# Prompt attention with operands split in pieces twelve steps ahead, its first pair loaded during decode, and the new tokens of the local sets multiplied together

## The chip, the cores and the metric

The program runs on one core of one Trainium2 chip, and its time is the device time of one execution in microseconds (us). The core has TensorE (PE, with its weight loads shown as PEld), VectorE (DVE), ScalarE (ACT), GpSimd (POOL) and SyncE (SP), which issues nearly all the transfers here. Each engine works through its own list of instructions in order and waits on semaphores that the others raise.

## What is computed

One layer of a hybrid decoder: a prompt of 512 positions, and 8 sequences of 8 new tokens with 4096 cached positions each. Both go through an input projection, attention in four sets of heads (one forgetting attention, "FOX", and three dilated sliding windows, "WIN", that are merged by their softmax denominators), gates and an MLP.

```python
q_f, k_f, v_f, logf, dil, ga, gb = project(h_p, pos_p, lp)
o_fox = fox_prompt(q_f, k_f, v_f, logf)
for g, ((w, r), (q, k, v)) in enumerate(zip(DIL_PATTERNS, dil)):
    o, lse = dilated_prompt(q, k, v, w, r)
h_p = finish(h_p, o_fox, merge_groups(outs, lses), ga, gb, lp)
...
q_f, k_f, v_f, logf, dil, ga, gb = project(h_s, pos_s, lp)
k_past = cache_fox_k[l][page_table].reshape(DB, past, N_HEADS_FOX, HEAD_DIM)
v_past = cache_fox_v[l][page_table].reshape(DB, past, N_HEADS_FOX, HEAD_DIM)
o_fox = fox_sample(q_f, k_f, v_f, logf, k_past, v_past, f_past)
o, lse, new_buf = dilated_sample(q, k, v, win_caches[g][l], w, r)
h_s = finish(h_s, o_fox, merge_groups(outs, lses), ga, gb, lp)
```

## The kernel before

The kernel has four parts, one after another, with a barrier of all engines between them: `project_tokens`, `attend_sample` (the decode part), `attend_prompt` and `finish`. To keep float32 accuracy every operand of a matmul is split into a high and a low part (`x_hi` by a copy on ACT, `x_lo` = x minus `x_hi` on DVE or POOL), and a product is made of two or three matmuls.

**Decode part.** For each of the 8 sequences ("batches") the cache is worked through in 24 groups: 16 FOX groups of 256 positions and 8 WIN groups (sets 1, 2, 3) of 128 or 256 gathered positions. `straight` writes the stages of each engine out by hand: at step n (24 steps for a batch) PE turns the keys of group n (L1211), turns probabilities of group n-21 (L1188), scores group n-2 (L1227) and sums values of group n-22 (L1242); SP loads keys for n and values for n-20, into rings of 6 slots each. The 8 new tokens of a sequence are appended to the last group of each of the four sets (`group_new`: groups 15, 16, 18 and 23). For such a group PE also turns an 8-column piece of `prob` (L1191) and adds two matmuls of 8 rows by 512 columns from `vn_hi` and `vn_lo` (the last loop of `sum_values`). POOL loads `vn_hi` and `vn_lo` once a batch, in two transfers. The FOX output and the merged WIN output of a batch are scaled on DVE (`out_rows`), turned on PE (`turn_out`, L1203) and copied into `o_t` (`out_diagonal`). After the last one SP stores `o_t` to `o_s` and waits for it.

**Prompt part.** The heads are taken in 4 pairs. A pair is 32 chunks: 2 heads, 4 query tiles, 4 sets in `SET_ORDER`; a chunk has 1 to 4 key tiles of 128. The steps of the `stream` of each engine are chunks too: PE scores chunk n-4 (L1599), turns the probabilities of chunk n-16 (L1611) and weighs the values of chunk n-18 where the query tile is the last (L1632). DVE keeps and masks the scores of chunk n-5 (L1554), takes the maximum and its negative (L1565, L1567), makes reciprocals and `pt_lo` (L1579). ACT takes exponentials (L1490), normalises FOX (L1497) and makes `pt_hi` (L1505); POOL normalises WIN (L1451). There are three banks for scores and three for turned probabilities, so PE can be at most three chunks ahead of DVE. The operands of a pair are split at fixed steps of it, four and more steps ahead of their use:

```python
if i in (0, 8):
    ...
    ve.tensor_tensor(q_lo[rows, hh], q_raw[rows], q_hi[rows, hh].bitcast(F32), ALU.subtract).then_inc(q_split, 1)
if 1 <= i <= SETS:
    ...
    ve.tensor_tensor(k_lo[:, s], k_raw[:, s], k_hi[:, s].bitcast(F32), ALU.subtract).then_inc(k_split, 1)
```

ACT does the `_hi` parts at the same steps (L1474, L1479) and `v_hi` at step 18 (L1483), POOL `v_lo` (L1444). `k_hi` and `k_lo` have one buffer, so a set's keys for the next pair can be split only when its last chunk (28 to 31) has been scored. At the start of the part SP loads `q_raw` and `k_raw` of the first pair (1 MB each), the biases, `causal`, `masks`, the values and two slabs for `finish`, in that order; the stored decode outputs come back into `o_all` last.

## Time and profile before

| | |
|---|---|
| median of 3 runs | 1935.24 us (1931.7 to 1937.51) |
| the profiled execution | 1934.01 us, span 1932.2 us |
| mean granted TensorE clock | 0.961 |
| busy share PE, DVE, ACT, POOL | 92%, 57%, 49%, 43% |

The table is the whole program; the parts differ, so a table by stage is among the rows below. The span is what the trace covers, 1.8 us less than the execution's own time. A busy PE is not PE at its peak, since the ends of matmuls are modelled; the distance between the starts of two matmuls is what one costs.

### The profile page before, as it was taken

What the parts mean: (1) busy time and instruction counts of PE and PEld (TensorE: products, weight loads), DVE (VectorE), ACT (ScalarE), POOL (GpSimd) and SP (SyncE); (2) the same over time, 40 slices, a digit from 0 to 9 for tenths busy, and PEclk for the clock granted to TensorE, in tenths of its full rate; (3) what the DMA queues carried; (4) which work ended last, traced back from release to release, by engine and by line L of the source; (5) the groups of instructions that cost most, each with busy time, mean ns of one, the idle gap of its engine ahead of it and who ended that gap; (6) DMA issues with size and microseconds to landing.
All of it is one profiled execution on the core that took longest, in us unless ns stands there. A gap on an engine that the chain in (4) does not pass through costs nothing. (4 is left out here: it accounts for less than half of the span.)

```text
span 1932.2 us, 33076 instructions
## 1 busy us (share of the span) xinstructions
PE 1771.0 (92%) x10797; PEld 1556.2 (81%) x10797; DVE 1107.8 (57%) x2535; ACT 954.2 (49%) x1608; POOL 830.4 (43%) x449
## 2 busy tenths in 40 slices
PE   7999999999599999999999947877799799999998
PEld 5787787899587888888888726777698799989897
DVE  6745646230487877878787847676552442415251
ACT  5434334331376877777777736666522322212130
POOL 2523324200156867867768633333333133333331
PEclk9999999999799999999999978888899999999999
DMA  6344362633899999999999754456254466666663
GB/s 219 101 158 141 114 209 74 203 119 88 237 341 320 326 332 339 319 332 334 323 330 335 261 173 155 136 182 217 83 177 172 182 226 233 259 260 239 234 244 114
DMA packets 225314, 427.12 MB, mean 221 GB/s; under 512 B 24521, under 2 KB 85834, under 8 KB 223506
## 3 DMA queue, kind: packets, MB, share of 16 engines
q1 hardware_dynamic: 224306, 423.15, 65.3%
q0 software_dynamic: 864, 2.10, 0.5%
q8 instruction: 84, 1.38, 0.3%
q14 instruction: 60, 0.49, 0.1%
HBM read 392.63 MB, written 119.86 MB: 265 GB/s over the span
## 5 line engine op out<-in xcount | busy, mean ns | idle before, releaser
L995 POOL TENSOR_TENSOR vv_lo<-v_raw,vv_hi 128x1024 fp32r<-128x1024 f32 x178 | 400.6, 2255 | 181.1 <-ACT vv_hi L1059 176.5
L1759 POOL TENSOR_TENSOR w_lo<-w_raw,w_hi 128x2048 fp32r<-128x2048 f32 x39 | 180.8, 4636 | 338.1 <-ACT w_hi L1774 338.1
L1051 ACT ACTIVATE kt_hi<-ktp 128x1024 fp32r<-128x1024 f32 (+1 forms) x192 | 186.2, 970 | 112.7 <-PE ktp L1211 110.4
L1075 DVE TENSOR_TENSOR kt_lo<-ktp,kt_hi 128x1024 fp32r<-128x1024 f32 (+1 forms) x192 | 220.4, 1148 | 9.8 <-ACT kt_hi L1051 9.4
L1211 PE MATMUL ktp<-ident,k_raw 128*128 128x128 f32 x1440 | 194.2, 277 | 19.8 <-DMA k_raw<-in_cache_fox_k 19.5
L1211 PEld LDWEIGHTS ktp<-ident,k_raw 128*128 128x128 f32 x1440 | 166.9, 143 | 51.0 <-DMA k_raw<-in_cache_fox_k 22.5
L1227 PE MATMUL s_ps<-kt_hi,q_st 128*128 128x256 f32 (+3 forms) x768 | 205.3, 301 | 0.4 <-DVE mx_parts L1107 0.4
L663 PE MATMUL acc<-w_hi,xn_hi 128*128 128x512 f32 x480 | 194.1, 404 | 2.4 <-POOL w_lo L302 2.4
L1059 ACT ACTIVATE vv_hi<-v_raw 128x1024 fp32r<-128x1024 f32 (+1 forms) x192 | 191.5, 997 | 6.4 <-PE o_ps L1242 6.0
L1227 PE MATMUL s_ps<-kt_lo,q_st 128*128 128x256 f32 (+3 forms) x768 | 190.0, 281 | 0.0
L663 PE MATMUL acc<-w_lo,xn_hi 128*128 128x512 f32 x480 | 189.4, 395 | 0.0
L1774 ACT ACTIVATE w_hi<-w_raw 128x2048 fp32r<-128x2048 f32 x40 | 76.6, 1915 | 202.2 <-PE acc L1953 156.4
L1953 PE MATMUL acc<-w_hi,right_hi 128*128 128x512 f32 x400 | 156.6, 392 | 0.0
L1953 PE MATMUL acc<-w_lo,right_hi 128*128 128x512 f32 x400 | 156.2, 391 | 0.0
L663 PE MATMUL acc<-w_hi,xn_lo 128*128 128x512 f32 x384 | 152.4, 397 | 0.0
L1227 PEld LDWEIGHTS s_ps<-kt_hi,q_st 128*128 128x128 f32 x768 | 145.6, 190 | 5.1 <-issue 3.1
L1242 PE MATMUL o_ps<-vv_hi,pt 128*128 128x512 f32 x360 | 145.8, 405 | 2.6 <-POOL vv_lo L995 1.2
L1227 PEld LDWEIGHTS s_ps<-kt_lo,q_st 128*128 128x128 f32 x768 | 145.9, 190 | 0.0
L1242 PE MATMUL o_ps<-vv_lo,pt 128*128 128x512 f32 x360 | 142.8, 397 | 0.0
L1905 DVE TENSOR_TENSOR second<-first 128x576 f32<-128x576 f32 x32 | 87.3, 2727 | 94.8 <-ACT first L1824 94.8
L314 POOL TENSOR_TENSOR y_cos<-y_unit,rope_cg 128x512 f32<-128x512 f32 x40 | 51.7, 1293 | 203.3 <-DVE y_unit L564 194.8
L441 DVE TENSOR_TENSOR w_lo<-w_raw,w_hi 128x2048 fp32r<-128x2048 f32 x31 | 74.9, 2417 | 104.0 <-ACT w_hi L335 103.9
(231 smaller groups left out, 4214.3 us busy)
## 6 DMA issues: line engine op xcount, KB each, us to landing
k_raw<-in_cache_fox_k SPq DMA_DIRECT2D x256, 256.0 KB, 6.4
v_raw<-in_cache_fox_v SPq DMA_DIRECT2D x256, 256.0 KB, 5.2
out_win_kv_sample<-in_cache_win_kv SPq DMA_DIRECT2D x32, 2040.0 KB, 9.9
w_raw<-in_w_in SPq DMA_DIRECT2D x32, 1024.0 KB, 5.9
k_raw<-in_cache_win_kv SPq DMA_DIRECT2D x40, 512.0 KB, 10.9
v_raw<-in_cache_win_kv SPq DMA_DIRECT2D x40, 512.0 KB, 12.0
w_raw<-in_w_up SPq DMA_DIRECT2D x16, 1024.0 KB, 5.5
w_raw<-in_w_down SPq DMA_DIRECT2D x16, 1024.0 KB, 5.0
```

What stands on the lines that cost most here:

```text
L663: last = pe.matmul(acc[:, t, :], x[:, kk, t * P:t * P + P], w[:, k, :], start=(kk == 0 and i == 0), stop=(kk == KT - 1 and i == len(lots) ...
L995: gp.tensor_tensor(vv_lo[:, slot, 0:tiles, :], v_raw[:, i % RAW_RING, 0:tiles, :], vv_hi[:, slot, 0:tiles, :].bitcast(F32), ALU.subtract). ...
L1051: act.activation(kt_hi[:, slot, :, 0:n], ktp[:, i % 2, :, 0:n], ACT.Copy).then_inc(k_hi, 1)
L1059: act.activation(vv_hi[:, slot, 0:tiles, :], v_raw[:, i % RAW_RING, 0:tiles, :], ACT.Copy).then_inc(v_hi, 1)
L1075: ve.tensor_tensor(kt_lo[:, slot, :, 0:n], ktp[:, i % 2, :, 0:n], kt_hi[:, slot, :, 0:n].bitcast(F32), ALU.subtract).then_inc(k_lo, 1)
L1211: last = pe.transpose(ktp[:, i % 2, q, n * P:(n + 1) * P], k_raw[:, i % RAW_RING, n, q * P:(q + 1) * P], ident[:])
L1227: last = pe.matmul(s_ps[:, i % S_RING, 0:wide], w, x, start=(n == 0), stop=(n == len(lots) - 1))
L1242: last = pe.matmul(o_ps[:], w, x, start=(group_first(i) and n == 0), stop=(group_last(i) and n == len(lots) - 1))
L1759: gp.tensor_tensor(w_lo[:, slot, :], w_raw[:, slot, :], w_hi[:, slot, :].bitcast(F32), ALU.subtract).then_inc(slab_lo_done, 1)
L1774: act.activation(w_hi[:, slot, :], w_raw[:, slot, :], ACT.Copy).then_inc(slab_hi_done, 1)
L1905: ve.tensor_tensor(second[:, f % 2, :], first[:, f % 2, :], first[:, f % 2, :], ALU.mult).then_inc(u_squared, 1)
L1953: last = pe.matmul(acc[:, (5 * c + t) % 8, :], x[:, kk, t * P:t * P + P], w[:, k, :], start=(kk == 0 and i == 0), stop=(kk == KT - 1 and i ...
```

## The change

- Decode part: the new tokens of the three WIN sets stand together at the end of `s_win` and are multiplied once, with the last WIN group (24 rows); those of FOX with group 15. `pt[:, :, 2]`, `vn_hi` and `vn_lo` have 128 rows, of which the unused ones are zeroed once, so both matmuls and the transpose use all rows. `scores_sum` has a second reduction for groups 16 and 18. The DVE stage that copies the outputs moves to the front of its step, PE's `turn_out` from the front of a step to the end of the one before.
- `o_t` outlives the decode part; POOL copies it into `o_all`. The store to `o_s` and the load of it are gone.
- `q_raw` and `k_raw` are one tile `qk_raw` that spans both parts. SP loads the first pair at the end of its decode list, the half tile of the first head, the keys, the half of the second head.
- Prompt part: all stages but the splits are 12 steps later in their pair. Queries, keys and values are split set by set: queries of head 0 at steps 0 to 3 (low part on POOL), keys at 13 to 16 (low part on POOL), queries of head 1 at 18 to 21 (low part on DVE), values at 27 to 30 (POOL). The first pair's queries of head 0 and keys are split at the start, low parts on DVE. DVE makes the negative maximum in one instruction.
- SP's list is written out for the four pairs, with its loads in another order; `finish` uses `qk_raw` for three of its tiles.

```diff
-OUT_TURN_BEHIND = 24
+OUT_TURN_BEHIND = 23
...
             def sum_values(b, i):
...
-                if group_new(i):
-                    lots += [(pt[0:DEC_SEQ, i % PT_RING, 2, :, :].rearrange("p x n -> p (x n)"), x[:, group_set(i), :]) for x in (vn_hi, vn_lo)]
+                if group_last(i):
+                    lots += [(pt[:, i % PT_RING, 2, :, :].rearrange("p x n -> p (x n)"), x[:, group_kind(i), :]) for x in (vn_hi, vn_lo)]
...
             def scores_sum(b, i):
...
+                if group_new(i) and not group_last(i):
+                    done(ve, p_done, group_index(b, LAST) - PER_BATCH)
...
-            sp.wait_ge(o_out, 2 * DEC_BATCH + 1)
-            for kind in (FOX, WIN):
-                sp.dma_start(a["o_s"][kind].rearrange("q p n -> p q n"), o_t[:, kind]).then_inc(o_stored, 16)
-            sp.wait_ge(o_stored, 32)
+            load_query_half(sp, a, qk_raw, pair_in, 0, 0)
+            load_pair_keys(sp, a, qk_raw, pair_in, 0)
+            load_query_half(sp, a, qk_raw, pair_in, 0, 1)
...
-SCORE_BEHIND, KEEP_BEHIND, EXP_P_BEHIND, RECIP_BEHIND, NORM_BEHIND = 4, 5, 6, 7, 8
-TURN_BEHIND, LOW_BEHIND, WEIGH_BEHIND, COPY_BEHIND = 16, 17, 18, 19
+SCORE_BEHIND, KEEP_BEHIND, EXP_P_BEHIND, RECIP_BEHIND, NORM_BEHIND = 16, 17, 18, 19, 20
+TURN_BEHIND, LOW_BEHIND, WEIGH_BEHIND, COPY_BEHIND = 28, 29, 30, 31
+Q_AT, K_AT, V_AT = (0, 18), 13, 27
...
+            def split_lo(p, i):
+                first = isinstance(p, int) and p == 0
...
+                j = i - K_AT
+                if 0 <= j < SETS and not first:
+                    s = SET_ORDER[j]
+                    gp.wait_ge(k_split_hi, pieces(p, j))
+                    gp.tensor_tensor(k_lo[:, s], k_raw[:, s], k_hi[:, s].bitcast(F32), ALU.subtract).then_inc(k_split, 1)
...
+            def queries_lo(p, i):
+                j = i - Q_AT[1]
+                if 0 <= j < SETS:
+                    s = SET_ORDER[j]
+                    ve.wait_ge(q_split_hi[1], pieces(p, j))
+                    ve.tensor_tensor(q_lo[64:128, 1, s], q_raw[64:128, s], q_hi[64:128, 1, s].bitcast(F32), ALU.subtract).then_inc(q_split[1], 1)
...
-                ve.tensor_reduce(mx[:, kind:kind + 1], mx_parts[:, kind, 0:parts], AX.X, ALU.max).then_inc(mx_done, 1)
-                ve.wait_ge(mx_done, unit(p, i) + 1)
-                ve.tensor_scalar(neg_mx[:, kind, qt:qt + 1], mx[:, kind:kind + 1], -1.0, None, ALU.mult).then_inc(neg_done, 1)
+                ve.tensor_reduce(neg_mx[:, kind, qt:qt + 1], mx_parts[:, kind, 0:parts], AX.X, ALU.max, negate=True).then_inc(neg_done, 1)
```

On PE in the decode part, where the values of a middle WIN group with new tokens (group 18) are summed; before (`vn_hi`, `vn_lo` are the new tokens' values, `ktp` the turned keys):

```order
L1242 MATMUL o_ps<-vv_hi,pt 128x512
L1242 MATMUL o_ps<-vv_lo,pt 128x512
L1242 MATMUL o_ps<-vn_hi,pt 128x512
L1242 MATMUL o_ps<-vn_lo,pt 128x512
L1211 MATMUL ktp<-ident,k_raw 128x128 x8
L1188 MATMUL pt_ps<-ident,prob 128x128 x2
L1227 MATMUL s_ps<-kt_hi,q_st 128x264
```

and now, at the same place:

```order
L1285 MATMUL o_ps<-vv_hi,pt 128x512
L1285 MATMUL o_ps<-vv_lo,pt 128x512
L1253 MATMUL ktp<-ident,k_raw 128x128 x8
L1230 MATMUL pt_ps<-ident,prob 128x128 x2
L1269 MATMUL s_ps<-kt_hi,q_st 128x264
```

The two matmuls of new tokens are gone here, as at group 16; at groups 15 and 23 they stay.

On SP, from the last value loads of the decode part on (the two branches stand where one part ends and the next begins, with the barrier between them); before:

```order
L919 DMA v_raw<-in_cache_win_kv 128x512 x2
L951 DMA o_s<-o_t 128x4x64 x2
L793 UNCONDITIONAL_BRANCH
L1378 UNCONDITIONAL_BRANCH
L1384 DMA q_raw<-qt_s 128x4x512
L1381 DMA k_raw<-kt_s 128x4x512
L1392 DMA bias<-lc_s 128x512 x2
L1406 DMA causal<-in_c_causal 128x128
L1407 DMA masks<-in_c_masks 128x1280
L1388 DMA v_raw<-v_s 128x4x128 x4
```

and now:

```order
L947 DMA v_raw<-in_cache_win_kv 128x512 x2
L811 DMA qk_raw<-qt_s 64x4x512
L817 DMA qk_raw<-kt_s 128x4x512
L811 DMA qk_raw<-qt_s 64x4x512
L822 UNCONDITIONAL_BRANCH
L1426 UNCONDITIONAL_BRANCH
L1434 DMA bias<-lc_s 128x512
L1445 DMA causal<-in_c_causal 128x128
L1446 DMA masks<-in_c_masks 128x1280
L1434 DMA bias<-lc_s 128x512
```

Two megabytes have moved from behind the barrier to ahead of it, and the store of `o_t` is gone.

On POOL in the prompt part's loop, where the turn of a pair lies (`probs` rows are the WIN normalisations, the widest ones belong to the last two query tiles of head 1); before:

```order
L1451 TENSOR_TENSOR probs<-probs,r_den 128x384
L1451 TENSOR_TENSOR probs<-probs,r_den 128x768
L1457 TENSOR_TENSOR bias_diag<-bias,causal 128x512
L1451 TENSOR_TENSOR probs<-probs,r_den 128x1024
L1444 TENSOR_TENSOR v_lo<-v_raw,v_hi 128x2048
L1451 TENSOR_TENSOR probs<-probs,r_den 128x1280
```

and now:

```order
L1508 TENSOR_TENSOR probs<-probs,r_den 128x768
L1507 REGISTER_ALU
L1508 TENSOR_TENSOR probs<-probs,r_den 128x1024
L1496 TENSOR_TENSOR k_lo<-qk_raw,k_hi 128x512 x4
L1507 REGISTER_ALU
L1508 TENSOR_TENSOR probs<-probs,r_den 128x1280
```

The four pieces of `k_lo` now stand on POOL behind the 1024-wide normalisation of the old pair and ahead of the 1280-wide one.

## Rows read from the trace of the kernel before

**Rows 1.** Windows: length, busy us of each engine, PEclk, DMA share, GB/s.

```profile
600.00:1000.00 400.00, 392.53 (x2787) 342.17 (x2786) 320.38 (x890) 307.05 (x565) 298.62 (x182) 1.00 1.01 330
...
1139.00:1159.00 20.00, 0.00 (x0) 0.00 (x0) 3.74 (x3) 3.98 (x5) 10.45 (x5) 0.50 0.81 258
1159.00:1387.00 228.00, 182.75 (x1064) 163.01 (x1064) 160.24 (x647) 148.84 (x327) 78.71 (x43) 0.85 0.44 147
```

**Rows 2.** Timeline of PE, the WIN output turned in two successive batches.

```profile
863.33 0.43 PE L1203 MATMUL pt_ps<-ident,o_rows 64*128 64x64 f32 x4 [1.21 <-DVE pt L1116]
...
938.88 0.43 PE L1203 MATMUL pt_ps<-ident,o_rows 64*128 64x64 f32 x4 [1.20 <-DVE pt L1116]
```

**Rows 3.** Timeline of PE in the decode part: start, us, instruction.

```profile
703.36 0.22 PE L1191 MATMUL pt_ps<-ident,prob 64*8 64x64 f32 x1
703.50 0.39 PE L1227 MATMUL s_ps<-kt_hi,q_st 128*128 128x264 f32 x1
...
707.09 0.40 PE L1242 MATMUL o_ps<-vv_hi,pt 128*128 128x512 f32 x1
707.33 0.40 PE L1242 MATMUL o_ps<-vv_lo,pt 128*128 128x512 f32 x1
...
708.32 0.66 PE L1211 MATMUL ktp<-ident,k_raw 128*128 128x128 f32 x4
```

**Rows 4.** Windows of 10 us over one decode batch, columns as in rows 1.

```profile
877.00:887.00 10.00, 10.00 (x75) 9.20 (x74) 8.38 (x23) 8.48 (x14) 9.16 (x10) 1.00 1.06 316
...
917.00:927.00 10.00, 10.00 (x74) 8.74 (x72) 7.37 (x22) 6.80 (x16) 7.59 (x4) 1.00 0.98 330
927.00:937.00 10.00, 10.00 (x72) 8.63 (x71) 8.29 (x24) 8.34 (x15) 6.22 (x4) 1.00 0.92 285
```

**Rows 5.** Timeline of all engines between decode and prompt part.

```profile
1138.71 0.39 DVE L1167 COPY o_t<-pt_ps 64x32 f32<-64x32 f32 x2 [0.75 <-PE pt_ps L1203]
...
1142.98 0.38 SPq L1384 DMA_DIRECT2D q_raw<-qt_s  x1
...
1145.65 0.44 SPq L1407 DMA_DIRECT2D masks<-in_c_masks  x1
...
1155.36 2.28 DVE L1529 TENSOR_TENSOR q_lo<-q_raw,q_hi 64x2048 fp32r<-64x2048 f32 x1 [16.26 <-DMA masks<-in_c_masks]
...
1161.15 0.29 DVE L1554 CUSTOM_DVE_ANT_0 probs<-s_ps,bias_diag 128x128 f32<-128x128 f32 x1
```

**Rows 6.** Timeline of the prompt part at two pair boundaries.

```profile
1251.01 1.92 ACT L1474 ACTIVATE q_hi<-q_raw 64x2048 fp32r<-64x2048 f32 x1
...
1252.95 2.28 DVE L1529 TENSOR_TENSOR q_lo<-q_raw,q_hi 64x2048 fp32r<-64x2048 f32 x1 [3.45 <-ACT q_hi L1474]
...
1257.90 1.89 POOL L1451 TENSOR_TENSOR probs<-probs,r_den 128x1024 f32<-128x1024 f32 x1 [9.74 <-DVE r_den L1574]
...
1258.35 2.00 DVE L1533 TENSOR_TENSOR k_lo<-k_raw,k_hi 128x512 fp32r<-128x512 f32 x1 [0.34 <-ACT k_hi L1479]
...
1308.34 1.92 ACT L1474 ACTIVATE q_hi<-q_raw 64x2048 fp32r<-64x2048 f32 x1
```

**Rows 7.** Windows of 4 us behind a pair boundary, columns as in rows 1.

```profile
1256.00:1260.00 4.00, 1.06 (x4) 0.61 (x4) 3.63 (x9) 2.66 (x7) 1.89 (x1) 1.00 0.58 188
...
1268.00:1272.00 4.00, 0.65 (x6) 0.41 (x4) 2.68 (x4) 2.34 (x4) 0.00 (x0) 0.92 0.96 306
1272.00:1276.00 4.00, 3.82 (x15) 3.50 (x16) 3.86 (x19) 1.89 (x6) 0.83 (x1) 0.50 0.55 171
```

**Rows 8.** Groups of the prompt part, 1159 to 1387: busy, mean ns | idle before.

```profile
L1529 DVE TENSOR_TENSOR q_lo<-q_raw,q_hi 64x2048 fp32r<-64x2048 f32 x7 | 16.0, 2287 | 19.1 <-ACT q_hi L1474 19.1
L1533 DVE TENSOR_TENSOR k_lo<-k_raw,k_hi 128x512 fp32r<-128x512 f32 x16 | 15.7, 993 | 1.6 <-ACT k_hi L1479 1.6
...
L1567 DVE TENSOR_SCALAR neg_mx<-mx 128x1 f32<-128x1 f32 x64 | 9.8, 154 | 2.2
...
L1444 POOL TENSOR_TENSOR v_lo<-v_raw,v_hi 128x2048 fp32r<-128x2048 f32 x4 | 18.2, 4560 | 7.3 <-ACT v_hi L1483 7.2
```

More of the change, by code:

```diff
@@ L755, in group_index, with score_col, new_col, new_rows @@
     return b * PER_BATCH + i
+def score_col(i):
+    return sum(group_tiles(n) for n in range(N_GROUPS[FOX] * group_kind(i), i)) * P
+def new_col(i):
+    tiles = sum(group_tiles(n) for n in range(PER_BATCH) if group_kind(n) == group_kind(i))
+    return tiles * P + (NEW_PLACE[group_set(i)] * DEC_SEQ if group_kind(i) == WIN else 0)
+def new_rows(i):
+    return (DEC_SEQ if group_kind(i) == FOX else WIN_NEW) if group_last(i) else 0
 def late_values(b, i):
@@ L937, in load_keys @@
                     for part, x in enumerate((vs_hi, vs_lo)):
-                        sp.dma_start(a["vn_s"][part].rearrange("p s n -> p (s n)"), x.rearrange("p s n -> p (s n)").bitcast(F32)).then_inc(vs_stored, 16)
+                        for first, place, count in ((0, 0, 1), (3, 1, 1), (1, 2, 2)):
+                            dst = a["vn_s"][part, place:place + count].rearrange("s p n -> p s n")
+                            sp.dma_start(dst, x[:, first:first + count].bitcast(F32)).then_inc(vs_stored, 16)
             def load_values(b, i):
@@ L1299, in attend_prompt @@
         masks = sb("masks", [P, 2 * P + 2 * SEQ])
-        q_raw = sb("q_raw", [P, SETS, SEQ])
-        k_raw = sb("k_raw3", [P, SETS, SEQ])
+        q_raw, k_raw = (qk_raw[:, n].rearrange("p (s n) -> p s n", s=SETS) for n in range(2))
         v_raw = sb("v_raw3", [P, SETS, Q_TILES, P])
@@ L1460, in _ @@
-            gp.wait_ge(in_small, N_SMALL)
-            gp.wait_ge(zeroed, 4)
-            stream(gp, PAIRS, CHUNKS, (0, diagonals), (RECIP_BEHIND, normalise), (0, values_lo))
+                if i in (8, 24) and not (isinstance(p, int) and p == 0 and i == 8):
+                    mask_diagonal(p, i // 16)
+            for done_before in (k_split, q_split[0]):
+                gp.sem_inc(done_before, SETS)
+            for s in SET_ORDER:
+                for x in (q_hi, q_lo):
+                    gp.memset(x[64:128, 0, s].bitcast(F32), 0.0).then_inc(zeroed, 1)
```

300 lines of the change are left out of this document (174 added, 126 removed).

## The prediction

> **What bounds the kernel now.** I first cut the span into stages by the windows view, because the page's mean of 92% for PE mixes parts with different limits. In the decode part from 600 to 1000 us PE is busy 392.5 of 400 us at full clock, and the DMA share is 1.01 at 330 GB/s [rows 1]: two resources are full at once. Which one sets the pace is told by the timeline: the WIN output is turned at 863.33 and at 938.88, so a batch takes 75.55 us, and nearly all of that PE works back to back; its only longer wait inside is 1.2 us for DVE [rows 2]. The windows of one batch show that the transfers have a little air: a share of 1.06 at its start, 0.98 and 0.92 forty and fifty us later [rows 4]. So PE sets the pace and the transfers are close behind.
>
> Between the parts, from 1139 to 1159, PE does nothing at all [rows 1]. In the prompt part, 1159 to 1387, no engine is full (PE 183, DVE 160, ACT 149, POOL 79 of 228 us) and PE's clock averages 0.85 [rows 1]. There the bound is a ring: PE may be three chunks ahead of DVE, DVE waits for ACT, ACT for PE. A long instruction in one of them stops the others. The timeline shows it at the turn of a pair: ACT spends 1.92 us on `q_hi`, DVE stands 3.45 us idle for it and then spends 2.28 us on `q_lo` [rows 6]. PE is busy only 1.06 of the 4 us that follow, and 0.65 of 4 us at the second such place; its clock is 0.50 in the window after that [rows 7]. The same ACT instruction comes at 1251.01 and 1308.34, so a pair takes 57.3 us [rows 6].
>
> **Decode part.** What a group's new tokens cost on PE: the last ordinary value matmul starts 0.24 us after the one before (707.33 less 707.09), and the next kind of work starts at 708.32, 0.99 us after it; the two 8-row matmuls between thus take 0.75 us [rows 3]. The small turning takes 0.14 us to the next start (703.36 to 703.50) [rows 3]; with what it makes wait ahead of it I take 0.2. Four groups a batch: 4 x 0.95 = 3.8 us. Afterwards there are two such groups, with full rows: four matmuls, which I price like the ordinary ones at 0.24, and two turnings at 0.14, 1.24 us. Saved 2.6 us a batch, 21 us over eight. The unknown is whether a full-row matmul of new tokens costs 0.24 or again 0.375 (half of 0.75); at 0.375 the saving is 2.0 us.
>
> The matmul page of the Trainium skill ("TensorE: Matmul & The Clock Gate", Step-by-step: what each phase is for) says that the time follows the columns and that the number of rows doesn't matter. By that rule alone only four of eight 512-column matmuls go, 4 x 0.24 = 0.96 us a batch, and this term would be 8 us. The rows disagree: the two with 8 rows take 0.75 us where two with 128 rows take 0.48.
>
> The transfers cap it. If the share could be held at 1.06, a batch could shrink to 75.55 x 1.01 / 1.06 = 72.0 us, 3.6 us of room. But the window with 1.06 moves only 316 GB/s against a mean of 330 [rows 1, 4], so a full share does not mean more bytes, and by bytes the room could be nearly nothing. I take 2.0 us a batch as what gets through, **16 us** for the part; bounds 5 (transfers hold it) and 21 (they don't).
>
> At nothing I put the rest of this part. The two extra reductions on DVE for groups 16 and 18 replace two pairs of small copies, and DVE is busy 320 of 400 us [rows 1]. `scores_sum` of group 16 now waits for the exponentials of the last group of the batch before; behind it on DVE stands `pt_lo` work that PE needs a step later. ACT does that exponential in the same step, ahead of its key copy, which DVE waits for anyway; were it late, PE would lose its length once a batch. POOL issues four loads of new values instead of two; it is busy 299 of 400 us [rows 1]. The three memsets and the four more stores of `vn_s` fall into the start, where DVE waits.
>
> **Between the parts.** `o_t` is complete at 1139.1 and the prompt part's first load is issued at 1142.98 [rows 5]: store, landing and barrier take 3.9 us. Without the store I leave 1.1 us for the barrier, so the part starts near 1140.2. DVE can begin when `masks` have landed: issued at 1145.65, there at 1155.36, behind 2.0 MB of queries and keys, two biases and `causal` [rows 5]. Of some 3.3 MB that land in 12.4 us from the part's start, 1.0 MB stays ahead of it. In proportion that is 3.7 us; with a fixed latency I take 5.5 us, then 1.6 us for `bias_diag` on POOL. DVE's eight first pieces lie beside that. The first chunk is kept near 1147.5 instead of 1161.15 [rows 5]: **13 us** (10, if the pieces or POOL's memsets are later; 14). The queries and keys loaded ahead stand behind the last values on SP's list and delay nobody but themselves.
>
> **Prompt part.** Gains: (a) the two holes of a pair, 2.94 us (4 less 1.06) at three boundaries and 3.35 us (4 less 0.65) at four places [rows 7], 22 us; (b) `k_lo` leaves DVE at three boundaries, 12 x 0.99 us, and the negation is gone, 9.8 us [rows 8]; DVE is busy 70% of the part [rows 1], and I let half of these 22 us count, 11 us; (c) PE's clock falls behind the holes; raising its mean from 0.85 to 0.9 is worth 5% of 183 us, of which a third lies on the path, 3 us. Sum 36 us.
>
> Losses: (d) `k_lo` of the next pair is now on POOL at 4.56 / 4 = 1.14 us a piece [rows 8], and the first stands behind a normalisation of 1.89 us [rows 6]. The keys have one buffer, so this can't start earlier than before: PE wants the first piece two steps after POOL's step. 1.89 + 1.14 less two short steps of about 0.9 is 1.2 us, and each further piece asks 1.14 us where PE's step is about as long; I take 2.5 us at each of three boundaries, 7.5 us. (e) Twelve small pieces replace three long ones on ACT, and four replace one on DVE. A quarter of 1.92 us is 0.48 us; at 0.6 us a piece ACT does 1.4 us more in a pair, and with the pieces' own share of the path I take 6 us for the four pairs. Net 36 - 13.5 = **22 us**; bounds 8 (holes only half closed) and 35.
>
> **The sum.** 16 + 13 + 22 = 51 us off the profiled execution's 1934.0 us gives 1883 us. The median of before is 1.2 us above that execution, well inside the bounds. `finish` and `project_tokens` keep their instructions.
>
> **Rivals.**
> 1. As above: 1883 us, chance 0.40, with its own range of 1873 to 1893.
> 2. The transfers hold the decode part: they take the place of PE as the bound, PE waits for keys around the twelfth group of each batch, and the term is 5 us. For it: the share of 1.01 and the 316 GB/s at 1.06; against it: 0.92 and 0.98 later in the batch. 1934 - 40 = 1894 us, chance 0.20.
> 3. POOL holds the prompt part: the pieces that moved to it come late and the holes are half closed, the term is 8 us. 1934 - 37 = 1897 us, chance 0.19. For it: a DVE instruction on two SBUF tiles took 2.00 us where its group's mean is 0.99, while POOL ran from 1257.90 to 1259.79 [rows 6, 8], and POOL now gets some 12 pieces more in a pair. DVE's new `q_lo` pieces are of that kind; all 16 colliding at 1 us more would be 16 us. The Trainium skill ("GPSIMD Engine Reference", Specifications) says that GpSimd shares its SBUF interfaces with VectorE, which contends where VectorE has two SBUF inputs; this row agrees.
> 4. The ring runs freely once the long instructions are gone, the clock stays up, and the prompt term is 35 us: 1870 us, chance 0.13.
> 5. Rivals 2 and 3 together: 1908 us, chance 0.05.
> 6. Slower than before: the single-buffered keys make POOL's chain at the turn of a pair the new wait. The other two terms give 29 us, so the prompt part would have to lose 29 us: with holes closed (36 less 6) the chain must stall 20 us at each of three boundaries where I take 2.5. That is longer than any run of POOL's rows; chance 0.03.
>
> **How the numbers follow.** A change of 0.3% (5.8 us) is about what a measurement of this kernel can tell from none. All cases but the last lie far on the fast side: faster 0.95, same 0.02, slower 0.03. The range goes from 1867 us (most of rival 4) to 1905 us (rivals 2 and 3 whole) and leaves out rival 5, the slow case and the far side of rival 4.
>
> **What would show it.** Right: a batch period near 73.5 us with no 8-row matmuls, the first kept chunk about 8 us behind the last copy of `o_t`, a pair period near 51 to 52 us, PE windows without a second hole. Wrong: PE waiting for `k_raw` in the steady decode part (rival 2), PE waiting for POOL's `k_lo` at a pair's first chunks for more than 3 us (rival 3 or 6), or a mean clock in the prompt part no better than 0.85.

## The result, and the profile after

The changed kernel takes 1907.12 us (median of 4 runs, 1902.44 to 1909.22), the kernel before 1935.31 us in the same session: a ratio of 0.985, 95% interval 0.983 to 0.988. It is faster by 28 us where 51 were forecast, outside the range of 1867 to 1905. The profiled execution took 1906.57 us, its span is 1904.8 us.

First the windows view of the kernel after, with the columns of [rows 1].

```profile
600.00:1000.00 400.00, 382.74 (x2774) 346.04 (x2773) 327.33 (x897) 310.37 (x569) 305.95 (x194) 0.99 1.01 333
...
1139.00:1159.00 20.00, 14.83 (x59) 11.77 (x58) 14.80 (x64) 13.60 (x34) 15.06 (x12) 0.64 1.15 361
1159.00:1387.00 228.00, 184.36 (x1134) 163.31 (x1135) 139.59 (x531) 148.57 (x336) 109.44 (x75) 0.90 0.51 155
```

In the decode part PE is busy 10 us less of 400 and the transfers still show a share of 1.01. The hole between the parts is filled. Next the timeline at this boundary, which answers to [rows 5]: the last copy of the output, the load of `masks`, and the first kept chunk.

```profile
1133.56 0.39 DVE L1209 COPY o_t<-pt_ps 64x32 f32<-64x32 f32 x2 [0.80 <-PE pt_ps L1245]
...
1135.91 0.42 SPq L1446 DMA_DIRECT2D masks<-in_c_masks  x1
...
1141.22 1.26 POOL L1512 TENSOR_TENSOR bias_diag<-bias,causal 128x512 f32<-128x512 f32 x1 [2.21 <-DMA masks<-in_c_masks]
...
1142.66 0.29 DVE L1637 CUSTOM_DVE_ANT_0 probs<-s_ps,bias_diag 128x128 f32<-128x128 f32 x1 [1.80 <-POOL bias_diag L1512]
```

These marks divide the gain by the three terms of the prediction:

| stretch, by the starts of | before | after | gained | forecast |
|---|---|---|---|---|
| span's start to last copy of `o_t` | 1138.71 | 1133.56 | 5.2 us | 16 |
| last copy to first kept chunk | 22.44 | 9.10 | 13.3 us | 13 |
| first kept chunk to last score | 207.9 | 199.7 | 8.2 us | 22 |
| the rest | | | 0.7 us | 0 |

The middle term is right. The other two have the sizes of rivals 2 and 3, which is rival 5: 1908 us at a chance of 0.05. What stood behind either size is another matter.

The table compares one trace with one. Three traces have the decode code of before (before, before_in_line, before_shift64) and six that of the changed kernel. The last copy starts at 1138.7 to 1141.9 us in the three and at 1131.9 to 1134.7 in the six, so the decode part gained 6.8 us by their means, and a difference of a few us between two single traces says little.

**The decode part after.** The waits view of PE from 600 to 1000 us: who waited, for whom, us in total, times, longest. Before, the first line read 6.0 us in 5 times (one a batch, [rows 2]), and there was no other.

```profile
PE pt_ps L1245 <- DVE pt L1158: 14.4, 11, 1.4
PE o_ps L1285 <- POOL vv_lo L1024: 2.3, 5, 0.5
```

The timeline of PE and DVE at a turning of the FOX output shows where the wait comes from.

```profile
683.38 0.40 PE L1285 MATMUL o_ps<-vn_hi,pt 128*128 128x512 f32 x1
683.62 0.40 PE L1285 MATMUL o_ps<-vn_lo,pt 128*128 128x512 f32 x1
683.85 1.03 PE L1253 MATMUL ktp<-ident,k_raw 128*128 128x128 f32 x8
...
686.11 0.40 PE L1285 MATMUL o_ps<-vv_lo,pt 128*128 128x512 f32 x1
...
687.36 0.28 DVE L1158 TENSOR_TENSOR pt<-pt_ps,pt 128x128 fp32r<-128x128 f32 x1
...
687.74 0.43 PE L1245 MATMUL pt_ps<-ident,o_rows 64*128 64x64 f32 x4 [1.23 <-DVE pt L1158]
```

Before, two 8-row matmuls of group 16 stood between the last value matmul and the turning, and DVE made its last `pt` piece under the second of them; PE turned the output without a wait:

```profile
685.72 0.39 PE L1242 MATMUL o_ps<-vn_lo,pt 8*128 8x512 f32 x1
...
685.76 0.28 DVE L1116 TENSOR_TENSOR pt<-pt_ps,pt 128x128 fp32r<-128x128 f32 x1
...
686.14 0.43 PE L1203 MATMUL pt_ps<-ident,o_rows 64*128 64x64 f32 x4
```

They are gone, and PE stands 1.23 us for that piece. The same comes once more before the WIN output is turned: 1.42 us at 786.81, where [rows 2] have 1.20. Windows of 2 us around this place show what can follow:

```profile
784.00:786.00 2.00, 1.39 (x7) 0.78 (x5) 1.90 (x4) 1.96 (x4) 1.56 (x2) 1.00 0.96 335
786.00:788.00 2.00, 1.10 (x9) 0.85 (x10) 1.39 (x7) 0.14 (x2) 1.91 (x1) 1.00 1.03 272
788.00:790.00 2.00, 2.00 (x11) 2.00 (x12) 1.94 (x7) 2.00 (x6) 0.28 (x1) 0.56 1.04 356
790.00:792.00 2.00, 2.00 (x9) 1.51 (x8) 0.73 (x2) 0.13 (x2) 2.00 (x1) 0.59 1.04 362
```

PE is busy only 1.39 and 1.10 of 2 us, and then the granted clock is 0.56 and 0.59, near the lower of its two levels, for some 4 us. The step there takes 4.4 us instead of 2.9. This happened in batches 1, 3, 5, 6 and 7, counted from 0, five of the seven in which the WIN output is turned. It isn't the gaps alone that decide it: in the run new_loads_apart below the same gaps (1.20 and 1.43 us) come in every batch, and the clock never falls in the decode part. Its windows at this place:

```profile
786.00:788.00 2.00, 1.02 (x8) 0.74 (x8) 1.39 (x7) 0.09 (x2) 2.00 (x1) 1.00 1.01 287
788.00:790.00 2.00, 1.97 (x14) 1.87 (x15) 1.94 (x7) 2.00 (x5) 0.17 (x2) 1.00 1.02 338
```

**The prompt part after.** DVE's timeline at the turn from pair 1 to pair 2, and behind it the transfers by queue from 1211 to 1315 us:

```profile
1211.96 0.27 DVE L1660 TENSOR_TENSOR pt_lo<-t_ps,pt_hi 128x128 fp32r<-128x128 f32 x1
...
1217.54 0.69 DVE L1637 CUSTOM_DVE_ANT_0 probs<-s_ps,masks 128x512 f32<-128x512 f32 x1 [5.31 <-issue]
...
1218.30 0.47 PE L1685 MATMUL s_ps<-k_hi,q_hi 128*128 128x128 f32 x1 [5.08 <-DVE mx_parts L1637]
```

```profile
q14 instruction: 10, 0.08, 0.3%
```

DVE stands 5.31 us with "issue" as the releaser: it waited for nothing that the profile shows. It stands there again 4.95 us one pair later. It is the place where the hardware loop over pairs 1 to 3 jumps back (the trace has DVE's branch at 1211.89 us), and in that stretch the core fetched ten pieces of instructions. The trace of before shows only one instruction transfer between 1240 and 1360, where its two jumps lie (1245.49 and 1302.99).

The other place is the turn from pair 0 to pair 1. SP, POOL and PE there:

```profile
1154.75 0.34 SPq L1434 DMA_DIRECT2D bias<-lc_s  x1
...
1160.53 14.28 SPq L1430 DMA_DIRECT2D v_raw<-v_s  x4
...
1179.16 1.29 POOL L1512 TENSOR_TENSOR bias_diag<-bias,causal 128x512 f32<-128x512 f32 x1 [10.69 <-DMA bias<-lc_s]
1180.41 3.32 POOL L1508 TENSOR_TENSOR probs<-probs,r_den 128x768 f32<-128x768 f32 x2
1183.68 2.49 POOL L1496 TENSOR_TENSOR k_lo<-qk_raw,k_hi 128x512 fp32r<-128x512 f32 x2
...
1185.19 0.47 PE L1685 MATMUL s_ps<-k_hi,q_hi 128*128 128x128 f32 x1 [4.96 <-POOL k_lo L1496]
```

A bias of 256 KB is issued at 1154.75 and POOL, which waits for it, goes on at 1179.16. Four value loads keep SP 14.28 us. What they meet are the window copies of pair 0, four of them, 5 MB, which the changed list of SP issues at 1145.72 us, ahead of the next keys. In the kernel before they stood behind all loads of the next pair:

```profile
1200.45 3.09 SPq L1400 DMA_DIRECT2D out_win_kv_sample<-in_cache_win_kv  x4
```

Behind POOL's wait stand two normalisations and the first `k_lo`, and PE stands 4.96 us for that.

### The profile page after: what moved, and what is told of

It is laid out like the page before. It is cut to its first block and busy times, and to the rows that moved or that the text cites. A ratio compares the mean times of both kernels' runs of the same rounds, so it can differ in the third digit from the quotient of the medians.

```text
span 1904.8 us, 33016 instructions
## 1 busy us (share of the span) xinstructions
PE 1752.0 (92%) x10749; PEld 1553.1 (82%) x10749; DVE 1093.7 (57%) x2474; ACT 957.0 (50%) x1644; POOL 871.8 (46%) x508
## 5 line engine op out<-in xcount | busy, mean ns | idle before, releaser
L441 DVE TENSOR_TENSOR w_lo<-w_raw,w_hi 128x2048 fp32r<-128x2048 f32 x31 | 74.9, 2419 | 104.1 <-ACT w_hi L335 103.9
```

## The experiments

Each run has a kernel of its own, as a difference to the changed kernel unless said otherwise. "Batch" is the mean length of decode batches 2 to 6, from the start of the first key turning of batch 2 to that of batch 7, divided by 5; the waits are PE's between 600 and 1000 us. In turn_later and few_rows the view gives further waits before the output turnings to "issue" (5.0 and 4.3 us), which the column leaves out.

| run | time, us | runs | ratio to before, 95% | batch | waits for DVE / keys |
|---|---|---|---|---|---|
| before | 1935.3 | 4 | | 75.55 | 6.0 / 0 |
| changed | 1907.1 | 4 | 0.985 (0.983 to 0.988) | 75.18 | 14.4 / 0 |
| turn_later | 1907.0 | 4 | 0.985 (0.982 to 0.988) | 75.79 | 8.7 / 5.0 |
| pt_first | 1903.8 | 4 | 0.984 (0.981 to 0.987) | 75.48 | 6.9 / 6.4 |
| new_loads_apart | 1905.6 | 4 | 0.985 (0.981 to 0.988) | 75.31 | 14.3 / 6.4 |
| few_rows | 1907.0 | 1 | | 75.65 | 7.1 / 3.8 |
| fewer_bytes | 1950.1 | 4 | 1.007 (1.005 to 1.009) | 82.81 | 6.9 / 32.8 |
| pt_first_skip | 1893.8 | 4 | 0.978 (0.976 to 0.980) | 73.43 | 7.2 / 0 |
| skip | 1901.5 | 4 | 0.983 (0.981 to 0.985) | 74.93 | 13.3 / 1.4 |
| code_in_line | 1893.4 | 4 | 0.978 (0.975 to 0.982) | 75.75 | 14.5 / 1.6 |
| windows_last | 1902.0 | 4 | 0.981 (0.980 to 0.983) | 74.89 | 14.6 / 0 |
| before_in_line | 1935.2 | 10 | 0.999 (0.998 to 1.000) | 75.71 | 6.0 / 0.6 |
| shift32 / 64 / 96 | 1898.6 / 1897.3 / 1906.7 | 1 each | | 75.26 / 75.81 / 75.33 | |
| before_shift64 | 1936.4 | 1 | | 76.14 | 6.0 / 1.0 |
| line_and_windows | 1891.0 | 5 | 0.976 (0.975 to 0.978) | 75.88 | 7.1 / 8.6 |
| all_and_new_apart | 1890.7 | 5 | 0.978 (0.976 to 0.979) | 75.06 | 7.1 / 8.1 |

The decode code of the changed kernel stands unaltered in six of these rows (changed, code_in_line, windows_last and the three shifts), and its batch reads 74.89 to 75.81 us there, 75.37 in the mean. A difference of half a microsecond between two rows is therefore no result.

**Decode: the wait for DVE.** Two ways to shorten PE's wait before it turns the output. The first turns it behind the next keys, on PE:

```diff
-            straight(DEC_BATCH, PER_BATCH, (0, turn_keys), (TURN_P_BEHIND, turn_probs), (2, score), (SUM_V_BEHIND, sum_values), (OUT_TURN_BEHIND, turn_out))
+            straight(DEC_BATCH, PER_BATCH, (0, turn_keys), (OUT_TURN_BEHIND, turn_out), (TURN_P_BEHIND, turn_probs), (2, score), (SUM_V_BEHIND, sum_values))
```

(with the numbers for a lag of 24, and DVE's `out_diagonal` behind `out_rows`). The second changes DVE's order:

```diff
-            straight(DEC_BATCH, PER_BATCH, (OUT_TURN_BEHIND + 1, out_diagonal), (1, keys_lo), (OUT_BEHIND, out_rows), (3, scores_low), (TURN_P_BEHIND, probs_hi), (3, scores_sum),
-                   (TURN_P_BEHIND, probs_lo), (3, maximum), (TURN_P_BEHIND, denominator), (EXP_BEHIND, values_lo))
+            straight(DEC_BATCH, PER_BATCH, (OUT_TURN_BEHIND + 1, out_diagonal), (1, keys_lo), (OUT_BEHIND, out_rows), (TURN_P_BEHIND, probs_hi), (TURN_P_BEHIND, probs_lo), (3, scores_low), (3, scores_sum),
+                   (3, maximum), (TURN_P_BEHIND, denominator), (EXP_BEHIND, values_lo))
```

> The changed kernel, with one thing moved: in the decode part PE turns the attention output behind the key turning of the next step instead of ahead of it. The trace of the changed kernel shows PE standing before both output turnings of a batch for DVE's last pt piece (1.4 and 1.2 us; before the change 1.2 once), and in batches 1, 3, 5 and 6 a clock of 0.56 to 0.59 right behind the second of these gaps (the step takes 4.3 instead of 2.9 us). Theory A (the gain on the new tokens came back as this wait, because the matmuls that covered it are gone): the key turning (1.0 us) now covers most of it, but PE must then wait some 0.5 us for DVE's copy of the output before it turns the next probabilities; gaps shrink from 2.6 to about 1.3 us a batch and the slow-clock steps go: a batch of 73 us in every batch, 10 to 16 us less than the changed kernel, about 1893. Theory B (the transfers hold the decode part): PE then waits for keys instead, batches stay at 74.2 and above, time 1907.

> The changed kernel, with DVE's order inside a decode step changed alone: it makes pt and its low part ahead of the two score operations instead of around them. Theory A (PE waits before the output turnings because DVE reaches the pt pieces late): the pieces are ready 0.8 us sooner (s_tmp 0.43 and s_fox 0.41 us now stand behind them), so the two gaps shrink from 1.4 and 1.2 to about 0.6 and 0.4 us, and the slow-clock steps behind the longer gap go: batches of about 72.7 us, some 12 us less than the changed kernel, about 1895. If the scores that now come later hold ACT's exponentials instead, little changes. Theory B (transfers hold it): batches stay at 74.2 and above, 1907.

Neither gave the 10 us that theory A wanted. The waits view of pt_first, 600 to 1000:

```profile
PE ktp L1253 <- DMA k_raw<-in_cache_fox_k: 6.4, 11, 1.4
PE o_ps L1285 <- POOL vv_lo L1024: 2.4, 5, 0.5
PE pt_ps L1245 <- DVE pt L1158: 2.3, 6, 0.4
```

DVE's wait at the turnings fell from 14.4 to 2.3 us (with its other waits for DVE 6.9 in all), and no slow clock follows it. In its place stands a wait for the key transfers, in the seventh to thirteenth step of most batches. One batch without such a wait took 73.38 us; the mean of five is 75.48. The wait that PE no longer does for DVE it does for the transfers: theory B. turn_later shows the same (5.0 us for keys), and its gaps moved in part to the copy of `o_t` (8.7 us).

**Decode: POOL's loads.** The four loads of new values stand behind each other on POOL. They take 0.54, 0.61, 0.52 and 0.57 us there, where two stood before; a step of PE rose from 2.97 to 3.66 us. The run issues one each at groups 7, 9, 11 and 13:

```diff
-                if i == 7:
...
+                if i in (7, 9, 11, 13):
+                    part, kind = divmod((i - 7) // 2, 2)
```

> The changed kernel, with POOL's four loads of new values issued at four different groups (7, 9, 11, 13) instead of all at group 7. In the changed kernel each issue takes POOL 0.52 to 0.61 us and PE's step 6 takes 3.66 us instead of 2.97, with a wait for vv_lo of 0.45 us. Theory A (POOL is nearly full here and two more issues in a row make PE wait): step 6 returns to 2.97, each batch is 0.7 us shorter, 5 us less than the changed kernel, about 1902. Rival: the step is slow for another reason or the transfers hold the part; then 1907.

The step is back at 2.97 from the third batch on, PE's wait for POOL is gone, and the time is the same within the intervals: PE now waits 6.4 us for keys.

**Decode: are rows free?** The value matmuls of the new tokens over the 8 or 24 rows that hold them:

```diff
-                    lots += [(pt[:, i % PT_RING, 2, :, :].rearrange("p x n -> p (x n)"), x[:, group_kind(i), :]) for x in (vn_hi, vn_lo)]
+                    lots += [(pt[0:new_rows(i), i % PT_RING, 2, :, :].rearrange("p x n -> p (x n)"), x[0:new_rows(i), group_kind(i), :]) for x in (vn_hi, vn_lo)]
```

> The changed kernel, with the four value matmuls of the new tokens taken over the 8 and 24 rows that hold them instead of all 128 (the zeroed rows are left out; same result). In the changed kernel a full-row one takes 0.24 us to the next start (683.38, 683.62, 683.85); before the change the pair of 8 rows took 0.75 us. Theory R (few rows cost more): the pair takes 0.6 to 0.75 us, PE's step 13 goes from 3.32 to about 3.6 us and step 21 from 2.97 to 3.2; since PE then waits for DVE anyway, the time stays within 2 us. Rival (columns alone count, and what was saved was the number of matmuls): the steps stay at 3.32 and 2.97.

PE's timeline in this run:

```profile
680.06 0.40 PE L1285 MATMUL o_ps<-vv_lo,pt 128*128 128x512 f32 x1
680.39 0.49 PE L1285 MATMUL o_ps<-vn_hi,pt 8*128 8x512 f32 x1
680.72 0.39 PE L1285 MATMUL o_ps<-vn_lo,pt 8*128 8x512 f32 x1
681.05 1.09 PE L1253 MATMUL ktp<-ident,k_raw 128*128 128x128 f32 x8
```

From start to start it is 0.33 us each (680.39, 680.72, 681.05), where the full-row ones of the changed kernel take 0.24 and 0.23 (683.38, 683.62, 683.85). The matmul ahead of the few-row ones pays too: the last full-row one has 0.33 instead of 0.24. The two steps of a batch rose from 3.32 to 3.68 and from 2.97 to 3.25 us; the steps behind them fell from 4.25 to 3.94 and from 4.61 to 4.31, since PE waits less there for DVE, and the time stays. Few rows cost more than full rows here; so the row of before was the better guide than the rule of the Trainium skill that the prediction weighed against it.

**Decode: the bytes.** To take the transfers' bound away, part of the value loads is left out from the second batch on. The first of three runs cuts every second FOX page of values to 64 rows:

```diff
+                        m = 64 if what == "V" and n == 1 and b > 0 else P
-                        sp.dma_start(raw[:, i % RAW_RING, n, :], src).then_inc(slots[i % RAW_RING], 16)
+                        sp.dma_start(raw[0:m, i % RAW_RING, n, :], src[0:m]).then_inc(slots[i % RAW_RING], 16)
```

> The kernel of pt_first (pt and its low part ahead of the scores on DVE), which from the second batch on loads only 64 of the 128 rows of every second value page of the FOX groups, 128 KB of 512 KB less in 16 groups of a batch, about 8% of the bytes; everything else runs as before on what stands in the buffer. In pt_first PE's waits for DVE were nearly gone, but PE waited for key transfers in groups 8, 10 and 12 of most batches (6.4 us between 600 and 1000), and its batches took 73.4 to 76.7 us. Theory B in its new form (with DVE's wait gone the transfers hold the part): no waits for keys, every batch 73.4 us or less, 12 us less than pt_first, about 1892. Rival (the waits for keys come from the order of issues or from single late transfers, not from the amount): they stay, 1904.

The expectation missed: fewer bytes, and 46 us slower than pt_first. Its windows line from 650 to 950 us, and that of pt_first below it:

```profile
650.00:950.00 300.00, 269.95 (x1892) 237.16 (x1891) 228.91 (x600) 212.48 (x384) 211.45 (x134) 0.98 0.98 279
```

```profile
650.00:950.00 300.00, 286.84 (x2070) 254.45 (x2070) 251.65 (x669) 231.76 (x422) 230.38 (x148) 1.00 1.02 331
```

The busy share hardly moves, the rate falls from 331 to 279 GB/s. Transfers into 64 rows do not relieve the ones into 128. So the next two leave out whole loads (one page of values in every odd FOX group), once with pt_first's order and once with that of the changed kernel:

```diff
+                        if what == "V" and n == 1 and b > 0 and i % 2 == 1:
+                            sp.sem_inc(slots[i % RAW_RING], 16)
+                            continue
```

> The kernel of pt_first with 8 of the 84 or so loads of 256 KB in a batch left out from the second batch on (the second value page of every odd FOX group; its tile keeps what stands there), all other transfers whole. The run fewer_bytes cut transfers to 64 rows instead, and the rate fell from 333 to 276 GB/s with the same busy share, so it did not lighten anything. Theory B (the bytes hold the decode part at about 75.3 us a batch on average, in the changed kernel and in every variant so far): with 8% fewer bytes no wait for keys, every batch 73.4 us or less (12.5 us off pt_first), about 1891. Rival (single late transfers or the order of issues): waits for keys stay, 1904.

> The changed kernel itself with the same 8 loads in a batch left out. It tells how much of the decode part's missing gain is PE's waiting for DVE, POOL and the slow clock behind the gaps alone, when the transfers hold nothing. Theory A: batches stay at 74.2 us, and those with the slow clock behind the second output turning at 75.2 to 76, so 1904 to 1907, and the difference to pt_first with the loads left out (12 us or so) is the price of the lost cover. Theory B alone (transfers cause it all): batches fall to 73 us and the time to about 1892.

The windows line of pt_first_skip from 600 to 1000:

```profile
600.00:1000.00 400.00, 389.36 (x2840) 350.91 (x2839) 345.37 (x923) 317.68 (x583) 312.01 (x196) 1.00 0.94 312
```

All five batches lie between 73.37 and 73.54 us and PE waits for no keys. With the order of the changed kernel and the same bytes, the mean is 74.93: 74.05 in two batches, 75.16 to 76.13 in the three behind whose turning the clock fell. So there are two bounds, one behind the other. PE's lost cover alone holds the part at 74.9 us. The bytes alone hold it at 75 to 76: 330 GB/s by 75.55 us before the change is 24.9 MB a batch, and at 333 GB/s, which no run with all its loads exceeded between 600 and 1000 us, that takes 74.9 us by this estimate. Only with both gone does the batch fall to 73.4. That the forecast had 73.5 is chance: it took 2.6 us off PE's work and let the transfers leave 2.0 of it, and here 3.5 came off, the transfers hold nothing, and POOL's loads and small waits take some back.

**Prompt: DVE's code.** DVE's instructions in line, first on the changed kernel, then, as a control, on the kernel before:

```diff
-            stream(ve, PAIRS, CHUNKS, (KEEP_BEHIND, keep), (KEEP_BEHIND, maximum), (RECIP_BEHIND, denominators),
+            straight(PAIRS, CHUNKS, (KEEP_BEHIND, keep), (KEEP_BEHIND, maximum), (RECIP_BEHIND, denominators),
```

> The changed kernel, with VectorE's instructions of the prompt part written out for all four pairs instead of a hardware loop over pairs 1 to 3; the other engines keep their loops. In the changed kernel DVE stands 5.3 us with nothing that it waits for at the turn from pair 1 to 2 and from 2 to 3 (at 1212.2 and again one pair later), and in both stretches two 8 KB transfers on an instruction queue lie inside; the kernel before shows no instruction transfer between 1244 and 1363 us. Theory C (the jump back of the loop makes DVE load code, and that is why the prompt part gained 8 us and not 22): both stretches go, a pair takes about 50 us instead of 55, and the time is 8 to 10 us less, about 1898. Rival D (DVE waits for something else there, such as a late transfer, or the same stall shows up on ACT's or PE's own jump): the stall stays and the time is 1907.

> The kernel before the change with VectorE's instructions of the prompt part written out for the four pairs instead of looped; a control for the run in line, which took 14 us off the changed kernel. Theory C1 (the stall at the loop's jump is new in the changed kernel; in the trace of before no instruction transfer lies between 1244 and 1363 us): nothing changes, 1935. Rival C2 (before the change the same jump cost as much and lay hidden in DVE's 3.5 us of waiting for ACT's q_hi): the last step of a pair falls from 4.8 us, and the time is 3 to 8 us less.

14 us on the changed kernel by the medians, of which the traces show 8.2 us between the first kept chunk and the last score (199.7 to 191.5 us), and nothing on the kernel before: theory C. The second half of pairs 1 and 2, from the score of chunk 16 to that of the next pair's chunk 0, takes 24.6 us instead of 28.3 to 28.7; the whole pairs 1 and 2 take 51.1 and 50.7 us where the prediction said 51 to 52.

What decides whether the jump stalls? The next runs only add semaphore increments in front of DVE's decode part, so that the same loop lies further on:

```diff
+            for _ in range(64):
+                ve.sem_inc(ahead, 1)
             for s in (k_lo, s_low, s_done, p_hi, p_lo):
```

> The changed kernel with 64 further semaphore increments ahead of DVE's decode part, where DVE waits anyway; they only move the place of DVE's later code by 64 instructions. Theory F (whether the loop's code must be loaded again at its jump depends on where its code lies): the two stalls of 5.3 us at the turns from pair 1 to 2 and 2 to 3 change or go, 1907 or some 10 us less. Rival (it depends on the loop's content alone): both stay at 5.3 us.

> The changed kernel with 32 further semaphore increments ahead of DVE's decode part (64 took both stalls at the loop's jump away, and no instruction transfer was left between 1210 and 1315 us). Theory F (place alone decides): the result is all or nothing, either 5.3 us at each of the two jumps and transfers in every pass, or neither; with a bound somewhere between 0 and 64, either is possible. Rival G (each further instruction ahead shifts the load a little and hides more of it): a stall of 2 to 3 us.

> The changed kernel with 96 further semaphore increments ahead of DVE's decode part. Theory F: all or nothing again, 1897 or 1907. Rival G: less or as much as at 64, so no stall, 1897.

> The kernel before the change with the same 64 semaphore increments ahead of DVE's decode part. Before, its loop of about the same length showed no instruction transfer after 1244 us and no gain from code in line. Theory F (place alone decides, for either loop): at this place the loop before may have to load its code in each pass, with instruction transfers in pairs 2 and 3 and up to 5 us more at each of two jumps, 1935 to 1946; if it stays clean, the bound lies elsewhere for it. Rival (something in the changed loop is needed): nothing changes, 1935.

With 32 and with 64 further instructions both stalls are gone; in shift64 no instruction transfer at all lies between 1211 and 1315 us. With 96 they are back, though shorter: DVE's timeline and its transfers from 1211 to 1315 in shift96:

```profile
1214.59 0.29 DVE L1663 TENSOR_TENSOR pt_lo<-t_ps,pt_hi 128x128 fp32r<-128x128 f32 x1
1218.51 0.69 DVE L1640 CUSTOM_DVE_ANT_0 probs<-s_ps,masks 128x512 f32<-128x512 f32 x1 [3.62 <-issue]
```

```profile
q14 instruction: 11, 0.09, 0.3%
```

So "all or nothing" was too simple: place decides whether code is fetched, and the stall is 5.3 us at one place and 3.6 at another. The kernel before, shifted by 64, now shows the same kind of fetches between 1240 and 1360 us:

```profile
q14 instruction: 11, 0.09, 0.2%
```

Its steps are none the longer (28.8 us for the half pair, as before; 1936.4 us in all). DVE's timeline behind the jump shows why. First the kernel before, its branch at 1245.49:

```profile
1247.92 0.56 DVE L1554 CUSTOM_DVE_ANT_0 probs<-s_ps,masks 128x384 f32<-128x384 f32 x1 [1.23 <-PE s_ps L1599]
...
1252.95 2.28 DVE L1529 TENSOR_TENSOR q_lo<-q_raw,q_hi 64x2048 fp32r<-64x2048 f32 x1 [3.45 <-ACT q_hi L1474]
```

Then the same shifted by 64, its branch at 1247.62:

```profile
1250.98 0.56 DVE L1557 CUSTOM_DVE_ANT_0 probs<-s_ps,masks 128x384 f32<-128x384 f32 x1 [2.03 <-PE t_ps L1614]
...
1255.23 2.28 DVE L1532 TENSOR_TENSOR q_lo<-q_raw,q_hi 64x2048 fp32r<-64x2048 f32 x1 [2.67 <-ACT q_hi L1477]
```

The records of DVE's sequencer give the stall itself: from the branch to the next register instruction it is 0.33 us in before and 3.00 us in before_shift64, as it is 0.33 in shift64 and 2.87 in the changed kernel (where a second piece follows). In before_shift64 DVE then starts its chunk 0.8 us later, and its wait for ACT's `q_hi`, a few instructions behind, is 0.8 us shorter. The two waits absorb the stall. The change took the second of them away, and with it the cover.

**Prompt: the window copies.** In SP's list the copies of a pair go behind the next pair's loads again, as before the change (they are 5 MB a pair; the 10 that the expectation names is wrong):

```diff
-                copy_windows(p)
+                if not more:
+                    copy_windows(p)
...
                     load_values(p + 1)
+                    copy_windows(p)
```

> The changed kernel, with the copies of the window caches (10 MB a pair) issued behind the next pair's queries, keys, bias and values in SP's list instead of ahead of its keys. In the changed kernel POOL stands 10.7 us for a bias (issued at 1154.75), the value loads take SP 14.3 us to issue, and PE waits 5.0 us for POOL's k_lo at the first chunk of pair 1. Theory E (the first pair's window copies, which now run while pair 1 is loaded, hold these loads and so the turn to pair 1): the last step of pair 0 (6.0 us) falls to about 1, pair 0 takes 43 us instead of 48, the time is about 1902. Rival: POOL's own chain of pieces is what is late (the 2.5 us a turn of the prediction): then the wait for k_lo stays at 4 us or more, 1907.

SP's list and PE's waits from 1170 to 1190 in this run:

```profile
1154.76 0.34 SPq L1434 DMA_DIRECT2D bias<-lc_s  x1
1160.64 2.05 SPq L1430 DMA_DIRECT2D v_raw<-v_s  x4
1162.73 2.50 SPq L1442 DMA_DIRECT2D out_win_kv_sample<-in_cache_win_kv  x4
```

```profile
PE s_ps L1687 <- POOL k_lo L1498: 1.5, 2, 1.2
```

The value loads take SP 2.05 us instead of 14.28, POOL's wait for the bias is gone, PE's for `k_lo` falls from 4.96 to 1.5 us, and pair 0 takes 44.5 us instead of 47.9. The time is 5 us less, theory E.

**Together.** Code in line, window copies last, pt first; then the four loads apart as well:

> The changed kernel with three edits together: DVE's prompt part in line (14 us less by itself), the window copies behind the next pair's loads (5 us less by itself), and pt ahead of the scores on DVE in the decode part (3 us less by itself). If they are independent: 1907 less 22 is about 1885. If the decode part is held by transfers either way, the third gives nothing: 1888. If the window copies without the stalls meet the next loads: 1893.

> The fastest kernel so far (code in line, window copies last, pt first; 1891) with POOL's four loads of new values issued at groups 7, 9, 11 and 13. Theory B (the transfers hold the decode part at a mean of 75 to 75.5 us a batch): step 6 falls from 3.66 to 2.97, the waits for keys grow by as much, and the time stays within 1 us of 1891. Rival A (what PE does counts): 0.7 us a batch, 5 us less, 1886.

1891.0 us, 44 us less than before and 16 less than the changed kernel: the fastest version with the whole computation. It is 6 us short of the plain sum. In the prompt part nothing is lost: from first kept chunk to last score it takes 187.3 us, 12.4 less than the changed kernel, and code_in_line and windows_last take 8.2 and 4.2 less. So the shortfall lies in the decode edit, which gives nothing (PE waits 8.6 us for keys), and in code_in_line's own 14 us, whose single runs varied from 1889 to 1899. The second edit changes nothing, as theory B says.

## Why the prediction was wrong

**Decode part (16 forecast, 5.2 measured).** Two steps failed, and either would have held the part by itself. The first is "I take 2.0 us a batch as what gets through". The part's own lower bound of 5 was the answer, and the working had the reason for it: a full share does not mean more bytes, so the room "could be nearly nothing". With PE's wait for DVE shortened, PE waits for keys instead, the rate stays at 333 GB/s and the batch at 75.5 us (pt_first). The row that the prediction gave for this, 316 GB/s at a share of 1.06, was a weak witness, though: in the same batch of before the window from 897 to 907 us has a share of 1.06 and 348 GB/s. In the profiled pair batches 2 to 6 gained 0.4 us each. 4.5 of the 5.2 us came from batch 7 and what drains behind it, where loads run out (121.0 us before from its first key turning to the last copy, 116.5 after); batches 2 to 6 gave 1.9 and the start lost 1.2.

The work saved on PE was undersized, not the reason. With the loads at hand and no slow clock, a batch of the changed kernel takes 74.18 us, 1.37 less. It has 1.45 us more wait before the two turnings (1.23 and 1.42 less 1.20) and 0.7 us more at POOL's loads, so PE has some 3.5 us less to do where 2.6 were forecast. The prices of a full-row matmul (0.24) and of short rows were right.

The second step that failed is "At nothing I put the rest of this part." It named POOL's four loads and DVE's order and gave them no price. Two costs sit there, the 1.45 and the 0.7 us, and the slow clock behind the longer wait adds 1.0 us to the mean batch (75.18 less 74.18). In the changed kernel's own trace it is these that hold PE: between 600 and 1000 us it never waits for keys. The cover that hid DVE's `pt` piece was the very work that the change removes. Had the prediction followed what PE does between the last value matmul and the turning, it would have seen two matmuls leave and a wait of 1.2 us, already there in [rows 2], grow. By skip, this alone would have held the part at 74.93.

**Between the parts (13 forecast, 13.3 measured).** Right by its steps: the part starts 1.5 us behind the last copy (1.1 forecast), POOL has `masks` 6.2 us later (5.5), and `bias_diag` takes 1.3 us (1.6); DVE waits for nothing else.

**Prompt part (22 forecast, 8.2 measured).** The gains were right as far as they went. The second hole is closed (step 6 of a pair's first half 4.44 us before, 1.23 after, 3.2 of the forecast 3.35), though the four steps behind it grew by 0.7, and the first halves of pairs 1 to 3 are 1.2, 2.3 and 1.6 us shorter. The last step of a pair went from 4.76 to 2.25. Loss (d) is 1.5 us a turn in windows_last, where 2.5 were taken. Rival 3's collision comes only in small part: the sixteen `q_lo` pieces on DVE have a median of 0.69 us, and six took 0.97 to 1.53, 3.0 us more in all where 16 were feared. The mean clock from first kept chunk to last score rose from 0.85 to 0.89, and line_and_windows, which has neither stall, lets the part gain 20.7 us, near the 22. What failed are two terms at which the sum put nothing:

- DVE's code at the loop's jump, 8 us in the traces (9 to 14 by the times). Step (a), "the two holes of a pair", took the time in which DVE waits for `q_hi` as free to win. Under it the stall of a fetch can be hidden (before_shift64), and a fetch comes or not by where the loop lies. In the trace of before that was not to be seen, since its jumps take 0.33 us. The Trainium skill ("Runtime: NRT & Kernel Launch", Instruction fetch mechanics) says that a taken branch whose target is no longer in the small window of loaded code must fetch it first. The trace agrees in kind, with 5.3 us for one such jump. By that rule this stall belonged among the rivals, and the prediction did not look at it; the rule alone would not have decided it, since the loop of before, of about the same length, jumps without a stall.
- The window copies, 5 us (4.2 in the trace). The change moved them ahead of the next keys in SP's list, from 1200.45 to 1145.72 us for pair 0, into the time in which pair 1 is loaded. The prediction priced what the engines do in the prompt part and never SP's list there; that step of the change is missing from it.

That the time came out within 1 us of rival 5's 1908 is no merit of rival 5. Its decode half was right in part: the transfers are a bound, but its sign, PE waiting for keys, shows only once the wait for DVE is shortened. Its prompt half, POOL's pieces, was wrong in cause and had the right size by chance.

## What to carry to other kernels

When two resources are full at once, work taken off one of them is worth what the other one leaves, and here the rate in GB/s told it while the busy share didn't. Before pricing an edit at nothing, ask whether the removed instructions were themselves the cover of a wait that stands behind them, and whether the wait that you remove is the cover of something else. Where a long loop jumps back, look for idle time without a releaser and for instruction transfers; writing the loop out, or moving it, is a cheap test.

## What the runs showed of the hardware

- A jump back of a DVE loop (294 records in the trace from branch to branch) cost 5.3 us, 3.6 us or nothing, with 0, 96, and 32 or 64 further instructions ahead of it. The fetches were 8 KB each, on an instruction queue.
- Cutting 16 of a batch's transfers from 128 to 64 rows lowered the rate from 331 to 279 GB/s at a share of 0.98.
- A value matmul of 512 columns over 8 rows takes 0.33 us from start to start, over 128 rows 0.24.
- Gaps of 1.2 and 1.4 us on PE within one batch were followed by about 4 us at a granted clock of 0.56 to 0.59 in five of seven batches of the changed kernel and in none of new_loads_apart; with 0.4 us there (pt_first) they never were. What decides it is open.
- Open too is which rule of place decides the fetch; four places were tried for the changed loop and two for that of before.
